# Levels of a triangular inverse: 64x64 quadrant products or 128x128 block-diagonal ones

## What is computed

```python
def step(s, inp):
    r_t, k_t, v_t, kk_t, a_t, w_t = inp
    sa = jnp.einsum("dbhij,dbhj->dbhi", s, kk_t)
    s = (s * w_t[..., None, :] - sa[..., :, None] * (kk_t * a_t)[..., None, :]
         + v_t[..., :, None] * k_t[..., None, :])
    y = jnp.einsum("dbhij,dbhj->dbhi", s, r_t) if readout else None
    return s, y
```

## Time and profile before

| | us |
|---|---|
| median of 3 runs | 2002.14 |
| the runs | 1995.63 to 2003.91 |
| the profiled execution | 2000.82 |
| its span in the trace | 1999.0 |
| granted TensorE clock, mean | 0.978 of 2.4 GHz |
| the recurrence, first level (1189.0) to the last product of `y` (1443.4) | 254.4 |

### The profile page before, as it was taken

One profiled execution on the slowest core, in us unless ns is written; L12 is line 12 of the kernel. 1 busy time (PEld: TensorE's weight loads), 2 busy tenths in 40 slices (PEclk: granted clock), 3 DMA queues, 4 the chain that ended last, 5 costly groups with the idle time before them and its releaser, 6 DMA issues.

```text
span 1999.0 us, 33611 instructions
## 1 busy us (share of the span) xinstructions
PE 1888.0 (94%) x13862; PEld 1002.9 (50%) x13862; DVE 767.7 (38%) x1549; ACT 476.9 (24%) x982; POOL 244.5 (12%) x292
## 2 busy tenths in 40 slices
PE   6999999999999999999899969888898999999997
PEld 2455775444444444434355438888743444444443
DVE  3551441111111100013332357766432888988001
ACT  3022552200000000033311544444322222221001
POOL 1150111000000000012000045455200000000000
PEclk9999799999999999999899989999999999999999
DMA  5422001233432223334311200000021222222222
GB/s 211 164 74 66 30 1 63 97 132 130 146 128 82 86 94 120 107 113 147 119 53 53 69 1 5 5 4 4 10 84 63 74 76 81 73 73 74 83 84 94
DMA packets 43861, 158.63 MB, mean 79 GB/s; under 512 B 5016, under 2 KB 5672, under 8 KB 42712
## 3 DMA queue, kind: packets, MB, share of 16 engines
q1 hardware_dynamic: 37440, 133.19, 20.1%
q10 hardware_dynamic: 6296, 23.58, 3.2%
HBM read 152.01 MB, written 6.31 MB: 79 GB/s over the span
## 4 chain that ended last, share of the span: by engine, by line
PE 88%; DVE 5%; ACT 5%; issue 1%; DMA 0%; ACTq 0%; POOL 0%; DVEq 0%; POOLq 0%
PE psum L330 47%; PE psum L1202 21%; PE psum L1987 2%; PE psum L1991 2%; PE psum L995 2%; PE psum L976 1%; PE psum L589 1%; DVE mem L2155 1%; PE psum L1152 1%; PE psum L963 1%; PE psum L1750 1%; PE psum L632 1%; PE psum L1342 1%; PE psum L1998 1%; DVE mem L2183 1%
## 5 line engine op out<-in xcount | busy, mean ns | idle before, releaser
L330 PE MATMUL psum<-mem 128*128 128x512 f32 (+1 forms) x2272 | 963.6, 583 | 29.3 <-DVE mem L483 14.2
L330 PEld LDWEIGHTS psum<-mem 128*128 128x128 f32 x2272 | 427.6, 190 | 535.7 <-issue 520.1
L1202 PE MATMUL psum<-mem 128*128 128x512 f32 x960 | 418.8, 595 | 4.1 <-DVE mem L2475 2.6
L1202 PEld LDWEIGHTS psum<-mem 128*128 128x128 f32 x960 | 180.8, 190 | 234.2 <-issue 226.7
L2556 DVE SCALAR_TENSOR_TENSOR mem<-mem 128x512 f32<-128x512 f32 x352 | 235.1, 748 | 0.0
L386 POOL TENSOR_TENSOR mem<-mem 128x512 f32<-128x512 f32 x24 | 30.4, 1269 | 1078.8 <-ACT mem L370 1078.4
L1987 PE MATMUL psum<-mem 64*64 64x64 f32 x1920 | 74.3, 223 | 13.4 <-DVE mem L2173 5.4
L1295 ACT ACTIVATE mem<-mem 128x512 f32<-128x512 f32 x22 | 13.9, 631 | 290.7 <-DVE mem L1311 290.6
L1231 DVE SCALAR_TENSOR_TENSOR mem<-psum,mem 128x512 f32 x16 | 12.0, 751 | 177.4 <-PE psum L1202 177.4
L1987 PEld LDWEIGHTS psum<-mem 64*64 64x64 f32 x1920 | 65.2, 137 | 19.3 <-DVE mem L2183 10.8
L1991 PE MATMUL psum<-mem 64*64 64x64 f32 x1920 | 71.5, 221 | 3.1 <-issue 2.8
(11 more groups left out here) (344 smaller groups left out, 1760.7 us busy)
## 6 DMA issues: line engine op xcount, KB each, us to landing
mem<-in_units SPq DMA_DIRECT2D x248, 512.0 KB, 3.4
mem<-in_cw ACTq DMA_DIRECT2D x2, 2048.0 KB, 10.4
mem<-in_wn ACTq DMA_DIRECT2D x1, 2048.0 KB, 9.0
bias_tiles<-bias_scratch ACTq DMA_DIRECT2D x1, 2048.0 KB
mem<-bias_tiles ACTq DMA_DIRECT2D x1, 2048.0 KB, 10.3
mem<-in_xT ACTq DMA_DIRECT2D x1, 2048.0 KB, 9.9
x_scratch<-mem ACTq DMA_DIRECT2D x1, 2048.0 KB, 8.7
mem<-x_scratch ACTq DMA_DIRECT2D x1, 2048.0 KB, 7.7
```

Of the source, the lines that this page charges most:

```text
L330: last = pe.matmul(dst, ring[:, slot, k, :], rhs(k), start=(k == 0), stop=(k == 7))
L1202: last = eng.matmul(ps[m % 4], ring[:, slot, k - 8 * part, :], rhs(k), start=(k == 0), stop=(k == ktiles - 1))
```

## The change

A level is no longer 8 products of 64x64 but 4 products of 128x128 weights. The two heads of a pair are the two diagonal blocks of a 128x128 weight matrix whose other two blocks are zero; the moving operand is the same 64 columns as before, both heads one above the other. For that A and Z get a layout of (pair, half, 64) with 128 columns a pair, where each half of the partitions fills its own half and the other is cleared once at the start (`clear`, and two memsets on VectorE). The inverse is kept as `Tt`: an odd level gives Z^T·Tt, is copied with a predicate into `Tt`, and the transpose goes to `T`. The masks of four levels are transposed to fit. A copy or a mask that writes A or Z now needs one instruction for each half of the partitions: `keep` 2 for 1; `mask_beta` 4 half ones for 4 (context), or 2 full and 4 half ones for 4 (latent); `first` 3 for 2. `fresh` is kept in X, so that G goes away.

```diff
 def level(n, d, it):
-                    if n % 2 == 0:
-                        each(lambda hp, c, t: eng.matmul(dst(E_[d], hp, t), g[t, hp, 1, :], T[t, hp, :], start=True,
-                                                         stop=True)).then_inc(q["made"], 1)
-                    else:
-                        a, b_ = (Tt, Z) if n < 9 else (Z, Tt)
-                        each(lambda hp, c, t: eng.matmul(dst(O_[d], hp, t), a[t, hp, :], b_[t, hp, :], start=True,
-                                                         stop=True)).then_inc(q["made"], 1)
+                    for hp in range(4):
+                        if n % 2 == 0:
+                            last = eng.matmul(full(E_[d], hp), A_[:, hp].rearrange("p a t -> p (a t)"), T[:, hp, :], start=True,
+                                              stop=True)
+                        else:
+                            last = eng.matmul(full(O_[d], hp), Z[:, hp].rearrange("p a t -> p (a t)"), Tt[:, hp, :], start=True,
+                                              stop=True)
+                    last.then_inc(q["made"], 1)
...
 def mask_beta(it):
-                    mask(BETA, "g1", 0, it, "beta_masked")
+                    for d in range(2):
+                        if lat(it):
+                            eng.tensor_tensor(split(st_[d]["g1"][it % 2]), wide(BETA[d], 0, 1)[:, :, :, 0],
+                                              bc22(masks[:, d, 0]), ALU.mult)
+                        for r in (ch(0), ch(1)):
+                            last = eng.tensor_tensor(split(own_half(st_[d]["A"][it % 2], r)), wide(BETA[d], 1, 1)[r, :, :, 0],
+                                                     bc22(masks[r, d, 1]), ALU.mult)
+                    last.then_inc(both["beta_masked"], 1)
...
 def grow(n, d, it):
+                    steps.did(eng.copy_predicated(split(Tt), bc22(kept), heads(O_[d])))
                     if n < 9:
-                        steps.link(eng.copy_predicated(split(T), bc22(kept), heads(O_[d])))
-                        eng.transpose(flat(Tt), flat(T)).then_inc(q["grown"], 1)
+                        steps.wait()
+                        eng.transpose(flat(T), flat(Tt)).then_inc(q["grown"], 1)
...
 def keep(n, d, it):
-                    eng.copy(split(s["Z"]), heads(E_[d])).then_inc(q["kept"], 1)
+                    for r in (ch(0), ch(1)):
+                        last = eng.copy(split(own_half(s["Z"], r)), heads(E_[d])[r])
+                    last.then_inc(q["kept"], 1)
...
 def first(d, it):
-                    steps.link(eng.tensor_tensor(Tt, s["g1"][it % 2][:, :, 1, :], view(lev[:, d, 0], 0, [[0, 4], [1, C]]),
-                                                 ALU.mult))
+                    for r in (ch(0), ch(1)):
+                        steps.link(eng.tensor_tensor(Tt[r], own_half(s["A"][it % 2], r), view(lev[r, d, 0], 0, [[0, 4], [1, C]]),
+                                                     ALU.mult))
```

More of the change, by code:

```diff
@@ L1871, in build @@
         kdsum = stage_take(NCH, 4, C)
+        in_yC = Region(yC.offset + 6 * G, yC.offset + NCH * 4 * C)
+        pairs_ = [dict(A=[r7.take(4, 2, C), stage_take(4, 2, C)], Z=in_yC.take(4, 2, C) if d == 0 else stage_take(4, 2, C)) for d in range(2)]
         st_ = []
@@ L1875, in build @@
                 cum=stage_take(4, C), tot=stage_take(4, C) if d else None, e2=stage_take(4, C),
[L1876 to L1879, removed]
+                dk=[dks.take(4) for _ in range(4)],
+                g1=[stage_take(4, C) for _ in range(2)], g2=[stage_take(4, 2, C) for _ in range(2)],
+                T=stage_take(4, C), Tt=[stage_take(4, C) for _ in range(2)], **pairs_[d],
+                bk=stage_take(4, 2, C), v=stage_take(4, C), X=stage_take(4, C), U=stage_take(4, C), M=stage_take(4, C)))
         DEC = math.exp(-0.5)
@@ L1955, in dst, with full, own_half @@
                 return psum[r, 2 * pair + hp // 2, lo:lo + width]
+            def full(at, hp):
+                pair, slot = at
+                return psum[:, 2 * pair + hp // 2, slot * P + (hp % 2) * C:slot * P + (hp % 2) * C + C]
+            def own_half(tile, r):
+                return tile[r, :, r.start // 64]
             def alpha(d, it):
@@ L2036, in y @@
                         g1, g2 = s["g1"][it % 2], s["g2"][it % 2]
-                        last = each(lambda hp, c, t: eng.matmul(dst(Y_[d], hp, c), s["U"][t, hp, :], g1[t, hp, 0, :],
+                        last = each(lambda hp, c, t: eng.matmul(dst(Y_[d], hp, c), s["U"][t, hp, :], g1[t, hp, :],
                                                                 start=True, stop=False),
@@ L2180, in grow @@
                     kept = lev[:, d, 1 + n // 2, :].bitcast(mybir.dt.int32)
+                    steps.did(eng.copy_predicated(split(Tt), bc22(kept), heads(O_[d])))
                     if n < 9:
-                        steps.link(eng.copy_predicated(split(T), bc22(kept), heads(O_[d])))
-                        eng.transpose(flat(Tt), flat(T)).then_inc(q["grown"], 1)
-                    else:
-                        eng.copy_predicated(split(Tt), bc22(kept), heads(O_[d])).then_inc(q["grown"], 1)
+                        steps.wait()
+                        eng.transpose(flat(T), flat(Tt)).then_inc(q["grown"], 1)
+                    else:
+                        steps.wait()
+                        eng.sem_inc(q["grown"], 1)
                 def add_x(it):
@@ L2215, in dve @@
                 scan(1, 1)
+                steps.link(eng.memset(st_[1]["Z"][ch(0), :, 1], 0.0))
+                steps.link(eng.memset(st_[1]["Z"][ch(1), :, 0], 0.0))
                 lay_first()
@@ L2264, in keep_fresh @@
                     for d in range(2):
-                        last = eng.copy(split(st_[d]["G"]), heads(G_[d]))
+                        last = eng.copy(split(st_[d]["X"]), heads(G_[d]))
                     last.then_inc(both["fresh_kept"], 1)
@@ L2375, in pool @@
                     first(d, 0)
+                for d in range(2):
+                    clear(st_[d]["A"][1])
                 for it in range(LAST + 1):
```

18 lines of the change are left out of this document (13 added, 5 removed).

## The result

The changed kernel takes 2199.64 us (median of 4 runs, 2197.97 to 2203.55), the kernel before 2000.95 in the same comparison (4 runs, 1995.63 to 2003.91): a ratio of 1.100, 95% interval 1.097 to 1.103, or 199 us more. The direction was forecast, but the time lies 66 us above the upper end of the range. The profiled execution has a span of 2198.9 us.

What follows compares the result with a forecast made beforehand. TensorE was taken as near its bound in the recurrence. Latent iterations +58.5, iterations 1 to 4 +32.4, iteration 0 +8.7, tail +0.5 and start +3 gave +103 on 2000.8: 2104 us, range 2090 to 2120 (62%).

Steps and rivals of the forecast that it cites:

- What bounds the kernel: In the recurrence TensorE is near its bound, busy 219.0 of 245.5 us; the other engines have room.
- "issue" waits: Nine rows of TensorE weight-load waits in the recurrence, together 13.2 us, assumed to be instructions not arriving fast enough.
- The levels: Full-width records at 0.112 us each, paced by weight loads: 1.79 us a level, +8.7 us an iteration.
- The rival of fast loads: In levels, loads hide behind streaming, 0.058 us a record: not slower, 2000 us, or 1966 without change costs; 3%.
- The changes of tile shape: Switching between full-array levels and 64x64 quadrant blocks costs 0.34 us a pair, 99 pairs; bounds 0 and 0.45.
- The rival of free changes: Tile-shape changes cost nothing, vanishing into TensorE's waits, while about 8 us of waits come back: 2078 us; 15%.
- ScalarE, VectorE, GpSimd: Half copies take 0.37 us each, +3.7 us of ScalarE an iteration; copies, `grow` and longer masks mostly covered by levels.
- The wait for `grow(5)`: TensorE's wait for VectorE's `grow` of level 5, direction 0, behind `mask_beta` in latent iterations: shrinks to 0.1 us.
- The start: Before the first level, extra `first` operations and a wider `mask_beta(0)` delay direction 1; +3 us.
- The iterations: Recurrence after the change: latent iterations 30.6 us, iteration 11 29.4, iterations 1 to 4 26.9, iteration 0 26.4.
- the rival on the clock: Weight loads reduce the array's streaming, so the clock falls; a fifth of its work at 1.2 GHz adds some 50: 2155; 6%.

Runs made afterwards that it cites:

- the first experiment: Changed kernel plus 14 unread products (128x128 weights, 256 columns), 4 ahead of raw_beta(0) and 10 behind it: 2199.62 us, ratio 1.099.
- the two kernels that held the clock: Changed kernel plus unread 256-column products in iterations 0 to 4: four ahead of level 2 (2106.08 us); 4, 4, 2, 4, 4 ahead of even levels, 14 around raw_beta(0) (2132.19 us).

## Why the prediction was right in direction and wrong in size

**What bounds the kernel.** Right. The recurrence was near TensorE's bound, and work added there shows in full. The 13.2 us of "issue" waits, which I had put down to instructions that came too slowly as an assumption, shrank to 1.6 at full clock with half as many records in the levels. That fits, and is no proof.

**The levels.** Right. 0.111 us a record was forecast as 0.112, twice what 64 columns stream, so that the load of 128 columns sets the pace. The rival of fast loads is out.

**The changes of tile shape.** Mechanism right, size some 15% too high: about 0.29 us a pair for 0.34, over 99 pairs 5 us. The page of the Trainium skill that was cited there gives no price, and this is what the runs put beside it. The rival of free changes is out.

**ScalarE, VectorE, GpSimd.** The half copies take 0.369 us each, as forecast, and they are covered, as forecast, but only because levels are twice as long. On levels of before they cost 12 us, and with masks and `first` 27. The wait for `grow(5)` was forecast to shrink to 0.1, and is 0.75 in a latent iteration by the weight loads (4.5 us in 6) and 1.05 in iteration 3 at full clock: too small in the sum by some half a microsecond each, and the very wait behind which the clock fell in two kernels. The start, forecast at 3, shows as 0.5 (1189.51 for 1189.01) where levels at half clock may cover the rest; at full clock, in the first experiment, a wait of 1.22 stands behind the first level's first direction as well.

**The iterations.** At full clock a context iteration takes 26.6 us where 26.9 was forecast, and a latent one 29.8 where 30.6 was. All terms together give 2093 to 2097 us by the two kernels that held the clock, beside a forecast of 2104. So about half of the 199 us, some 95, is what the prediction had worked out.

**The step that failed is the rival on the clock.** It was named, with a mechanism that fits but that no run isolates ("with weights to load half of the time the array streams less"), and mis-sized twice: its chance (6%), and its price (+50 for a fifth of the work). It took place in every run of the kernel (mean granted clock 0.92 to 0.93 in all four), and cost some 102 us: iterations 1 to 4 take 47.5 to 49 us each at half clock against 26.6 at full, and iterations 0 and 5 carry the rest. The chance rested on the earlier trace rows, where a like mixture held 1.00 for 40 us. But that stretch has 282 records in 40 us, the first five iterations after 2382 in 246, and the records of the earlier trace rows are not of 64 columns alone. I had no row of the new mixture, and took the nearest one as proof. And a loop that does not bring the clock back pays on every turn until something else does, here iteration 5. A price for "a fifth" had no reason; the natural price was "until the mixture changes", 5 iterations of 12.

The Trainium skill (TensorE: Matmul & The Clock Gate, HAM oscillation — how this bites in real kernels) puts the loss of the clock down to waits that leave TensorE idle between its bursts. The falls in the recurrences traced here agree in kind: each stands within some 3 us behind a wait, of 0.9 to 2.0 us. What this doesn't cover is what followed in this kernel: in the first experiment its records leave no gap at all from 1191 to 1433, at a clock of 0.50. For that the measurement decides.

**What is shown and what stays open.** Shown: the context iterations of the kernel after do not bring the clock back, hold it at times but not surely, and with one long product more in each they do both. In every trace where the clock fell in the recurrence it fell just behind a wait. Such a wait is not enough, though: the 0.9 us of iteration 3 cost the clock in two kernels and not in the four that have long products in every context iteration. Only argued: that it is the small share of streaming beside the loads that keeps the clock down. The long product changes the streaming, the share of loads and the spacing of records at once, and no run separates these. No run takes the wait away either, which would show whether it is what tips the clock.

## What to carry to other kernels

Before small products are merged into full-width ones, compare the time to load the weights with the time to stream the columns: with 64 moving columns in float32 the load of 128 columns sets the pace at 0.111 us a record, and two quadrants side by side did the same work in half the time. Keep blocks of one tile shape together: each visit to another shape costs some 0.29 us. And when TensorE's mixture turns to short products with large weights, read the granted clock, not the busy share. If it is half, one long product in each turn of the loop shows cheaply whether the clock is the cause. And look at the short waits ahead of its falls: a wait that costs 1 us by itself stood ahead of 130 us at half clock.

## What the runs showed of the hardware that was not expected

TensorE can be busy by its records for 242 us without a gap and be granted half its clock all that time (the first experiment). One more product of 0.43 us in each iteration brought 1.00 back after 57 us, and it then stayed.

An operation on 64 partitions cost here about what one on 128 does: 0.369 us for a copy of 256 columns on ScalarE beside 0.37, and 0.738 on GpSimd, where the same line took 0.771 with 128 partitions in the kernel before:

```profile
L2353 POOL TENSOR_TENSOR mem<-mem 128x256 f32<-128x256 f32 x24 | 18.5, 771 | 52.1 <-DVE mem L2155 52.1
```
